# Merge gates of a two-block transformer layer: from direct matmuls to seven block products

## The chip, the cores and the metric

The kernel runs on one core of one Trainium2 chip. The metric is device time of one execution in microseconds (us). The kernel before took 1978.28 us as the median of three runs (1976.41 to 1979.21). Everything is float32.

## The reference, cut to what matters

Two transformer blocks run one after the other over 512 tokens of width 1024. The change lies in the second block, whose attention output `ya` and mLSTM output `ym` are merged by gates:

```python
h = rmsnorm_2(x, norm1_g[l])
proj = h @ w_in[l]            # its last 2048 columns are mg
...
gates = jax.nn.sigmoid(mg + merge_b[l])
u = gates[..., :D_MODEL] * (ya @ w_branch_attn[l]) + gates[..., D_MODEL:] * (ym @ w_branch_mlstm[l])
x = x + u @ w_out[l]
x = x + hier_moe(rmsnorm_2(x, norm2_g[l]), ...)
```

So `mg` is a product of a 512x1024 matrix (the tokens) and a 1024x2048 matrix (weights), and the kernel computes it transposed, as gate columns by tokens.

## The kernel before, in words

Each engine has its own instruction list, written out by hand and kept in order by semaphores. `hT` holds the normed tokens transposed: 8 blocks of 128 model columns by 512 tokens. Weights come in chunks of 2 MB (1024 rows by 512 columns) into a ring of two slots. SP's queue issues these loads in the order in which chunks are used, and each waits until TensorE is done with the chunk that had the slot (`chunk_done`, line 423).

The stage around the change runs in this order on TensorE. The window attention of the second block ends with the matmuls of line 1098. Then comes the mLSTM: `bcast_m`, `qk` and `num` (lines 1043 to 1066), for four heads in two directions, between which VectorE masks (line 2158), weighs (2167) and normalizes and adds (2175 to 2190), and ScalarE takes exponentials. Then `merge_gates(0)` (line 1130) computes the gate columns of output half 0 for both branches: two chunks, in each four groups of 8 matmuls of 128x128 weights by 512 tokens, one group a PSUM bank, which ScalarE reads through a sigmoid into `gates` (line 1580). Within it TensorE turns the two branch outputs (`turn(T_BR)`, line 729 for the transposes), which VectorE copies out (lines 1660 to 1663). Then the branch projections of half 0 (line 1156, two weights of 1 MB in one chunk), with VectorE forming the gated sum `merged` (lines 2224 to 2226). Then `merge_gates(1)` and the branch projections of half 1. The output projection (line 844 in `token_group`) adds to `x`; after it come a norm, the router, and 32 experts whose weights, 6 MB each, are loaded while the expert before is computed.

GpSimd (POOL) has next to nothing to do in this stage: at `hsum_done` 8, the end of the mLSTM, it issues three small DMAs (lines 653 to 655).

The MLP of the first block already uses the scheme that the change brings to the gates. `up_product` (line 860) and `down_product` (line 905) replace the eight products of 2x2 blocks by seven, P1 to P7, of sums of blocks. A product is 8 matmuls of 128x128 by 256. There VectorE forms the sums of weight blocks (for example line 1867, 128x1024 elements) and combines the products from PSUM (for example line 1961), and ScalarE copies P1 out of PSUM (line 1430).

Of the kernel before, what the change touches and what calls it, by code (L numbers as in the profile page):

```python
# [24 lines left out]
ALU = mybir.AluOpType  # L25
# [34 lines left out]
def build(nc, io, out):  # L60
    ctx = ExitStack()
    with ctx:
# [86 lines left out]
        merged = cbuf[:, 0:4096].rearrange("p (c t) -> p c t", c=8)  # L149
        gates = R[:, 0:4096].rearrange("p (b c t) -> p b c t", b=2, c=4)  # L150

# [115 lines left out]
        def kv_view(c):  # L267
# [43 lines left out]
            sem("num_done"), sem("hsum_done"))  # L311
        msq_done, mss_done, mstd_done, mnorm_done = sem("msq_done"), sem("mss_done"), sem("mstd_done"), sem("mnorm_done")
        gate_sig, u_done = sem("gate_sig"), sem("u_done")
        logits_done, r_exp, r_exp_done = sem("logits_done"), sem("r_exp"), sem("r_exp_done")
        h_store = [sem(f"h_store{s}") for s in range(2)]
# [167 lines left out]
        def _(sp):  # L483
# [85 lines left out]
            sp.wait_ge(turn_evac, 40)  # L569
            for j in range(3):  # L570
                sp.dma_start(views[0][j], source[j][0]).then_inc(loads[j][0], 16)

# [31 lines left out]
        def _(pool):  # L604
# [45 lines left out]


            pool.wait_ge(hsum_done, 8)
# [49 lines left out]
        def _(pe):  # L702
# [416 lines left out]
            pe.wait_ge(vext_done, 4)  # L1119
            pe.wait_ge(vone_done, 1)  # L1120
            bcast_m(0)
            qk(0)
            bcast_m(1)
            for r in range(8):
# [4 lines left out]
                num(r)  # L1129
            def merge_gates(half):  # L1130
                for br_ in range(2):
                    c = C_MERGE + 3 * half + br_
                    use_chunk(c)
                    for j in range(4):
                        gs = 8 * half + 4 * br_ + j
                        group(4 + gs % 4, gate_sig, gs + 1)
                        for k in range(KT):
                            ins = pe.matmul(ps[:, 4 + gs % 4, :], ring_view(c, KT, 512)[:, k, j * P:(j + 1) * P],  # L1138
                                            hT[:, k, :], start=(k == 0), stop=(k == KT - 1))
                        ins.then_inc(proj_done, 1)  # L1140
                        if half == 0 and br_ == 1 and j < 2:
                            turn(T_BR, [2 * j, 2 * j + 1])

            bo = 0
            for half in range(2):
                merge_gates(half)
                c = C_MERGE + 3 * half + 2
                pe.wait_ge(turn_evac, 40)
# [165 lines left out]
        def _(act):  # L1314
# [228 lines left out]
            act.wait_ge(acol_ready, 1)  # L1543
            for r in range(8):
                h, dr = r // 2, r % 2
                act.wait_ge(nmd_done, r + 1)
                if r >= 2:
                    act.wait_ge(num_done, r - 1)
                for j in range(NT):
                    a_col = colsb[:, 0, j, 32 * dr + h:32 * dr + h + 1]  # L1550
                    act.activation(E[:, r % 2, j, j * P:(j + 1) * P], nmd[:, r % 2, j, :], ACT.Exp, bias=a_col
                                   ).then_inc(wexp_done, 1)
                    lo, hi = ((j + 1) * P, 512) if dr == 0 else (0, j * P)
                    if lo < hi:
                        act.activation(E[:, r % 2, j, lo:hi], ps[:, 4 + r % 2, lo:hi], ACT.Exp, bias=a_col
                                       ).then_inc(wexp_done, 1)
            act.wait_ge(sig_done, 4)
            act.activation(sigT[:, :, :], sigT[:, :, :], ACT.Sigmoid).then_inc(sig_done, 1)
            act.wait_ge(hsum_done, 8)
            for a in range(NT + 1):  # L1560
                if a < NT:
                    if a >= 2:
                        act.wait_ge(mss_done, a - 1)
                    act.activation(stage[:, a % 2, 0:512], mix[:, a, 512:1024], ACT.Square).then_inc(msq_done, 1)
                if a >= 1:
                    act.wait_ge(mss_done, a)
                    at = 16 + 4 * (a - 1)
                    act.activation(hstd[:, at:at + 4], hss[:, at:at + 4], ACT.Sqrt, bias=epsc[:, 0:1], scale=1.0 / DM
                                   ).then_inc(mstd_done, 1)
            gs = 0  # L1570
            for half in range(2):
                for br_ in range(2):
                    for j in range(4):
                        bank = 4 + gs % 4
                        gs += 1
                        act.wait_ge(proj_done, len(G1) + len(G2) + gs)
                        if half:
                            act.wait_ge(u_done, j + 1)
                        b_ = 8 * br_ + 4 * half + j
                        act.activation(gates[:, br_, j, :], ps[:, bank, :], ACT.Sigmoid, bias=mergeb[:, b_:b_ + 1]  # L1580
                                       ).then_inc(gate_sig, 1)
            for a in range(NT + 1):
# [53 lines left out]
        def _(dve):  # L1636
# [533 lines left out]
            def head_sum(r):  # L2170
# [9 lines left out]
                for b_ in range(2):  # L2180
# [7 lines left out]
                    else:  # L2188
                        then(ins)
                        ins = dve.tensor_tensor(dst, dst, tmp, ALU.add)  # L2190
                        if b_ == 1:
                            ins.then_inc(hsum_done, 1)

            masked_m(0)
            for r in range(8):
# [6 lines left out]
            for a in range(NT + 1):  # L2202
                if a < NT:
                    dve.wait_ge(msq_done, a + 1)
                    at = 16 + 4 * a
                    dve.tensor_reduce(hss[:, at:at + 4], stage[:, a % 2, 0:512].rearrange("p (h e) -> p h e", h=4),
                                      AX.X, ALU.add).then_inc(mss_done, 1)
                if a >= 1:
                    i = a - 1
                    at = 16 + 4 * i  # L2210
                    dve.wait_ge(mstd_done, i + 1)
                    then(dve.reciprocal(hrs[:, at:at + 4], hstd[:, at:at + 4]))
                    mv = mix[:, i, 512:1024].rearrange("p (h e) -> p h e", h=4)
                    dve.tensor_tensor(mv, mv, bc(hrs[:, at:at + 4], DM), ALU.mult).then_inc(mnorm_done, 1)
            dve.wait_ge(sig_done, 5)
            for i in range(NT):
                take_turned(T_BR, i)
            for half in range(2):
                for j in range(4):
# [3 lines left out]
                    a_, b_ = merged[:, bo, :], stage[:, 0, (j % 2) * 512:(j % 2) * 512 + 512]  # L2223
                    dve.tensor_tensor(a_, gates[:, 0, j, :], ps[:, (2 * bo) % 4, :], ALU.mult)
                    then(dve.tensor_tensor(b_, gates[:, 1, j, :], ps[:, (2 * bo + 1) % 4, :], ALU.mult))
                    dve.tensor_tensor(a_, a_, b_, ALU.add).then_inc(u_done, 1)
# [218 lines left out]
```

## Time and profile before

| | us |
|---|---|
| median of 3 runs | 1978.28 |
| time of the profiled execution | 1978.18 |
| span of the profiled execution, first to last instruction | 1976.3 |
| merge gates (both halves) and branch projections, with their turns, 1096.13 to 1265.15 | 169.0 |
| mLSTM ahead of them, about 1037 to 1096 | 59 |

The profile is of one execution. A row that names an engine, a line and tiles gives a busy time. TensorE's rows (PE) come in pairs for float32: a matmul of the code is two records, of which each has its own duration, and they overlap. So the time that a run of matmuls takes is read from the chain of waits, where each piece has its start and its length, and not from the sum of the busy times.

### The profile page before, as it was taken

How to read it: one execution, taken by the hardware profiler on the slowest of the kernel's cores; microseconds unless marked ns; L12 is line 12 of the kernel's file. 1: busy time of each engine (PE TensorE's matmuls, PEld its weight loads, DVE VectorE, ACT ScalarE, POOL GpSimd, SP SyncE). 2: the span in 40 equal slices, each digit the busy share in tenths (PEclk: the TensorE clock that was granted, in tenths of full speed). 3: DMA queues.
4: the chain of work that ended last, by engine and by line, in shares of the span. 5: the costliest groups of instructions: out<-in, count | busy, mean ns of one | idle time of the engine just before them, and what ended most of it. 6: DMA issues, size and time to landing. Idle time of an engine off the chain costs nothing.

```text
span 1976.3 us, 23885 instructions
## 1 busy us (share of the span) xinstructions
PE 1867.3 (94%) x9785; PEld 1062.6 (54%) x9785; DVE 754.6 (38%) x1554; ACT 367.2 (19%) x794; POOL 63.5 (3%) x106
## 2 busy tenths in 40 slices
PE   7999999999999999999998999995999999999994
PEld 3344466568888888654555544454444444444441
DVE  3375666355445343535436220133222222222223
ACT  3332265210000000224434200010111111111110
POOL 0000000000000000100000000000000000000002
PEclk9999968999999999998998899995999999999997
DMA  3532100250222223120111112431999999999994
GB/s 119 119 93 85 69 17 1 85 176 1 85 86 86 90 94 114 55 95 34 43 44 42 57 54 74 191 149 67 355 394 389 387 378 396 398 398 393 392 402 153
DMA packets 83824, 329.17 MB, mean 167 GB/s; under 512 B 7895, under 2 KB 9044, under 8 KB 75564
## 3 DMA queue, kind: packets, MB, share of 16 engines
q1 hardware_dynamic: 71964, 287.45, 38.4%
q0 software_dynamic: 7632, 26.11, 4.9%
q10 hardware_dynamic: 4160, 14.68, 1.9%
q8 instruction: 46, 0.75, 0.2%
q14 instruction: 22, 0.18, 0.0%
HBM read 305.41 MB, written 22.81 MB: 166 GB/s over the span
## 4 chain that ended last, share of the span: by engine, by line
PE 88%; DMA 5%; DVE 3%; ACT 2%; issue 1%; POOL 0%; SPq 0%; POOLq 0%; DVEq 0%; ACTq 0%
PE ps L1212 10%; PE ps L869 10%; PE ps L913 10%; PE ps L761 7%; PE ps L1008 6%; PE ps L844 6%; PE ps L1138 6%; PE ps L1220 5%; PE ps L1240 5%; DMA W<-in_w_expert_up 4%; PE ps L768 3%; PE ps L1156 3%; PE ps L1247 2%; PE ps L797 2%; PE ps L820 1%; PE ps L1019 1%
## 5 line engine op out<-in xcount | busy, mean ns | idle before, releaser
L1212 PE MATMUL ps<-W,yT 128*64 128x512 f32 x1024 | 229.4, 601 | 3.0 <-DMA W<-in_w_expert_up 1.9
L1212 PEld LDWEIGHTS ps<-W,yT 128*64 128x64 f32 x1024 | 72.6, 138 | 144.9 <-issue 143.5
L761 PE MATMUL ps<-hT,W 128*128 128x512 f32 (+1 forms) x336 | 148.4, 600 | 2.2 <-DVE hT L1666 1.3
L1008 PE MATMUL ps<-hT,W 128*128 128x512 f32 x272 | 126.2, 619 | 0.7 <-ACT gb L1467 0.7
L1220 PE MATMUL ps<-W,yT 128*32 128x256 f32 x2048 | 117.1, 380 | 0.0
L1240 PE MATMUL ps<-W,yT 128*64 128x512 f32 x512 | 116.9, 598 | 0.0
L2362 DVE COPY mix<-ps 32x256 f32<-32x256 f32 x128 | 53.9, 421 | 153.7 <-PE ps L1247 152.4
L1138 PE MATMUL ps<-hT,W 128*128 128x512 f32 x256 | 111.2, 595 | 0.0
L761 PEld LDWEIGHTS ps<-hT,W 128*128 128x128 f32 (+1 forms) x336 | 63.0, 190 | 85.2 <-issue 81.9
L1220 PEld LDWEIGHTS ps<-W,yT 128*32 128x32 f32 x2048 | 63.3, 110 | 64.4 <-issue 26.0
L2343 DVE TENSOR_TENSOR yT<-yT,ps 64x512 f32<-64x512 f32 x32 | 22.1, 691 | 193.2 <-ACT yT L1598 193.2
L869 PE MATMUL ps<-yT,cbuf 128*128 128x256 f32 x384 | 85.6, 379 | 2.4 <-issue 2.4
L1008 PEld LDWEIGHTS ps<-hT,W 128*128 128x128 f32 x272 | 53.3, 200 | 63.5 <-issue 62.7
L913 PE MATMUL ps<-cbuf,mix 128*128 128x256 f32 x368 | 81.9, 379 | 0.0
L1138 PEld LDWEIGHTS ps<-hT,W 128*128 128x128 f32 x256 | 48.8, 192 | 60.2 <-issue 60.2
L869 PEld LDWEIGHTS ps<-yT,cbuf 128*128 128x128 f32 x384 | 72.9, 190 | 12.4 <-issue 2.6
L913 PEld LDWEIGHTS ps<-cbuf,mix 128*128 128x128 f32 x368 | 69.9, 190 | 9.5
L1430 ACT ACTIVATE smb<-ps 128x512 f32<-128x512 f32 x10 | 6.0, 595 | 352.6 <-PE ps L913 185.3
L1598 ACT ACTIVATE yT<-ps 64x512 f32<-64x512 f32 x32 | 18.9, 590 | 270.3 <-PE ps L1212 270.3
L1240 PEld LDWEIGHTS ps<-W,yT 128*64 128x64 f32 x512 | 33.9, 136 | 57.0 <-issue 54.8
L1364 ACT ACTIVATE ptb<-ps 32x512 f32<-32x512 f32 x82 | 48.3, 588 | 85.5 <-PE ps L761 84.8
L1247 PE MATMUL ps<-W,yT 128*32 128x256 f32 x1024 | 61.9, 382 | 0.0
(357 smaller groups left out, 2535.3 us busy)
## 6 DMA issues: line engine op xcount, KB each, us to landing
W<-in_w_expert_gate SPq DMA_DIRECT2D x32, 2048.0 KB, 17.8
W<-in_w_expert_up SPq DMA_DIRECT2D x32, 2048.0 KB, 22.3
W<-in_w_expert_down SPq DMA_DIRECT2D x32, 2048.0 KB, 23.4
W<-in_w_in SPq DMA_DIRECT2D x16, 2048.0 KB, 7.7
W<-in_w_up SPq DMA_DIRECT2D x8, 2048.0 KB, 7.5
W<-in_w_down SPq DMA_DIRECT2D x8, 2048.0 KB, 8.0
y_scratch<-mix ACTq DMA_DIRECT2D x32, 384.0 KB, 9.3
W<-in_w_out SPq DMA_DIRECT2D x4, 2048.0 KB, 8.0
```

What stands on the lines that cost most here:

```text
L761: ins = pe.matmul(ps[0:n, bank, :], wv[:, k, j * P:j * P + n], hT[:, k, :], start=(k == 0), stop=(k == KT - 1))
L768: ins = pe.matmul(ps[:, bank, :], hT[:, k, j * P:(j + 1) * P], wv[:, k, :], start=(k == 0), stop=(k == KT - 1))
L844: ins = pe.matmul(ps[:, bank, :], lhs[:, k, i * P:(i + 1) * P], ring_view(c, KT, 512)[:, k, :], start=(k == 0), stop=(k == 7))
L869: ins = pe.matmul(ps[:, bank, 256 * j:256 * j + 256], lhs[:, k, j * P:(j + 1) * P], rhs[:, k, :], start=(j == 0 and k == 0), stop=(j == 1 ...
L913: ins = pe.matmul(ps[:, bank, 256 * t:256 * t + 256], lhs[:, k, t * P:(t + 1) * P], rhs[:, k, :], start=(q == 0 and t == 0 and k == 0), st ...
L1008: ins = pe.matmul(ps[:, bank, :], wv[:, k, j * P:(j + 1) * P], hT[:, k, :], start=(k == 0), stop=(k == KT - 1))
L1138: ins = pe.matmul(ps[:, 4 + gs % 4, :], ring_view(c, KT, 512)[:, k, j * P:(j + 1) * P], hT[:, k, :], start=(k == 0), stop=(k == KT - 1))
L1156: ins = pe.matmul(ps[:, bank, :], ring[c % 2][:, br_ * 2048 + k * 512 + j * P:br_ * 2048 + k * 512 + (j + 1) * P], yT[:, 4 * br_ + k, :], ...
L1212: ins = pe.matmul(ps[64 * part:64 * part + 64, 2, :], xsT[:, x_slot, k, 0:64], wviews[s][part][:, k, :], start=(k == 0), stop=(k == KT - 1))
L1220: ins = pe.matmul(ps[32 * q:32 * q + 32, 3, 0:256], xsT[:, x_slot, k, 64:BLK], wviews[s][q // 2][:, k, 256 * (q % 2):256 * (q % 2) + 256], ...
L1240: ins = pe.matmul(ps[64 * half:64 * half + 64, 4, :], hTa[:, k, :], wviews[s][2][:, k, half * 512:(half + 1) * 512], start=(k == 0), stop= ...
L1247: ins = pe.matmul(ps[32 * q:32 * q + 32, 5, 0:256], hTb[:, k, :], wviews[s][2][:, k, q * 256:(q + 1) * 256], start=(k == 0), stop=(k == 3))
```

## The change: seven products for each chunk of gates, their sums on GpSimd, and all gates first

The gates of a chunk (512 gate columns by 512 tokens, 1024 deep) are computed as seven products of 2x2 blocks, 56 matmuls of 128x128 by 256, where it was 32 of 128x128 by 512. The four sums of weight blocks of each chunk (`gate_w_sums`) and four sums of token blocks, once (`gate_h_sum`), are formed by GpSimd. The token sums may start once the window attention is done; the weight sums of chunk 0 follow them at once. ScalarE copies P1 and P5 from PSUM, VectorE combines the products into the gate's tile (`gate_post`), and ScalarE applies the sigmoid there, in SBUF. The four chunks are now all computed ahead of the branch projections, and the turns of the branch outputs lie behind the third chunk and two products later. On SP's queue the loads of the four gate chunks go before the two of the branch weights, and a wait for `gate_read` 28 stands ahead of the second load of expert weights. The squares of the mLSTM's norm use other halves of `stage` and other semaphores. Some of it, cut:

```diff
+        def gate_view(c):
+            base = cbuf if c < 2 else R
+            return base[:, 2048 * (c % 2):2048 * (c % 2 + 1)].rearrange("p (j t) -> p j t", j=4)
...
-                chunk_done[C_MERGE + 3 * half + br_] = (proj_done, len(G1) + len(G2) + 8 * half + 4 * (br_ + 1))
-            chunk_done[C_MERGE + 3 * half + 2] = (y_done, 8 + 4 * (half + 1))
+                chunk_done[C_MERGE + 2 * half + br_] = (gate_prod, 7 * (2 * half + br_ + 1))
+            chunk_done[C_MERGE + 4 + half] = (y_done, 8 + 4 * (half + 1))
...
+        GATE_READ = dict(P2=1, P6=2, P3=4, P7=5, P4=7)
+        def gate_bank(n):
+            return 4 + n % 4
...
             for half in range(2):
-                c = C_MERGE + 3 * half
-                load(c, cols_of(w2, MG + 512 * half, 512))
-                load(c + 1, cols_of(w2, MG + D + 512 * half, 512))
-                c += 2
+                for br_ in range(2):
+                    load(C_MERGE + 2 * half + br_, cols_of(w2, MG + D * br_ + 512 * half, 512))
+            for half in range(2):
+                c = C_MERGE + 4 + half
                 sp.wait_ge(*chunk_done[c - 2])
+                if half:
+                    sp.wait_ge(y_done, 9)
...
+            def gate_h_sum(n, a, b):
+                pool.tensor_tensor(gate_h[n], a, b, ALU.subtract).then_inc(t_sums, 1)
+                pool.wait_ge(t_sums, 37 + n)
+            def gate_w_sums(c):
+                wv = ring_view(C_MERGE + c, KT, 512)
+                a11, a12, a21, a22 = (wv[:, 4 * k:4 * k + 4, 256 * n:256 * n + 256] for n in range(2) for k in range(2))
+                s1_, s2_, s4_ = gate_w[c // 2]
+                pool.wait_ge(ring_load[(C_MERGE + c) % 2], 16 * ((C_MERGE + c) // 2 + 1))
+                if c % 2:
+                    pool.wait_ge(gate_prod, 7 * c - 1)
+                pool.tensor_tensor(s1_, a21, a22, ALU.add).then_inc(w_sums, 1)
+                pool.wait_ge(w_sums, 64 + 4 * c + 1)
+                pool.tensor_tensor(s2_, s1_, a11, ALU.subtract).then_inc(w_sums, 1)
+                pool.wait_ge(w_sums, 64 + 4 * c + 2)
+                pool.tensor_tensor(s4_, a12, s2_, ALU.subtract).then_inc(w_sums, 1)
+                pool.wait_ge(gate_prod, 7 * c + 3)
+                pool.tensor_tensor(s1_, a11, a21, ALU.subtract).then_inc(w_sums, 1)
+                pool.wait_ge(w_sums, 64 + 4 * c + 4)
...
+            pool.wait_ge(pv_done, len(units))
+            pool.wait_ge(scan_done, 1)
+            gate_h_sum(0, b12, b11)
...
+            for c in range(2):
+                gate_w_sums(c)
+            pool.wait_ge(num_done, 8)
+            pool.wait_ge(wexp_done, 56)
+            gate_w_sums(2)
             pool.wait_ge(hsum_done, 8)
...
+            gate_w_sums(3)
...
+            def gate_product(n):
+                c, name = n // 7, PRODUCTS[n % 7]
+                bank = gate_bank(n)
+                use_chunk(C_MERGE + c)
...
+                if name == "P1":
+                    lhs, rhs = wv[:, 0:4, 0:256], hT[:, 0:4, 0:256]
+                    group(bank, gate_kept, 2 * c + 1)
+                elif name == "P5":
+                    lhs, rhs = w_s[0], h_s[0]
+                    pe.wait_ge(w_sums, 64 + 4 * c + 1)
...
+                for j in range(2):
+                    for k in range(4):
+                        ins = pe.matmul(ps[:, bank, 256 * j:256 * j + 256], lhs[:, k, j * P:(j + 1) * P], rhs[:, k, :],
+                                        start=(j == 0 and k == 0), stop=(j == 1 and k == 3))
+                ins.then_inc(gate_prod, 1)
...
+            for n in range(14):
+                gate_product(n)
+            for n in range(14, 21):
+                gate_product(n)
+            turn(T_BR, [0, 1])
+            for n in (21, 22):
+                gate_product(n)
+            turn(T_BR, [2, 3])
+            for n in range(23, 28):
+                gate_product(n)
...
+            for c in range(4):
+                for n in (7 * c, 7 * c + 2):
+                    gate_keep(n)
+                gate_sigmoids(c, False)
+                gate_sigmoids(c, True)
...
+            for n in range(0, 21):
+                gate_post(n)
             dve.wait_ge(sig_done, 5)
             for i in range(NT):
                 take_turned(T_BR, i)
+            for n in range(21, 28):
+                gate_post(n)
```

`gate_keep` is ScalarE's copy of P1 or P5 (128x512 from PSUM). `gate_sigmoids` are two sigmoids of 128x512 at a time. `gate_post` is one VectorE addition of 128x512 for each of P2, P3 and P4 (a bank of PSUM with a tile of SBUF), and two for P6 and P7, the second of which has both inputs in SBUF. P5 waits for the first weight sum of its chunk, P6 for the second, P3 for the third and P7 for the fourth. The order in a chunk is P1, P2, P5, P6, P3, P7, P4.

## Rows read from the trace of the kernel before

**Rows 1.** The page: busy time by engine, and the chain's shares by engine.
```profile
PE 1867.3 (94%) x9785; PEld 1062.6 (54%) x9785; DVE 754.6 (38%) x1554; ACT 367.2 (19%) x794; POOL 63.5 (3%) x106
...
PE 88%; DMA 5%; DVE 3%; ACT 2%; issue 1%; POOL 0%; SPq 0%; POOLq 0%; DVEq 0%; ACTq 0%
```
**Rows 2.** The chain, gates and branches: start, length, engine, tile, line, records.
```profile
1096.13 35.01 PE ps L1138 x80
...
1139.76 1.75 PE ps L729 x16
...
1155.24 27.47 PE ps L1156 x64
1182.71 54.93 PE ps L1138 x128
```
**Rows 3.** The line of the gates' matmuls.
```profile
L1138 PE MATMUL ps<-hT,W x256: 592/592/1061, 1095.9 to 1237.1; 128*128 128x512 f32 x128
```
**Rows 4.** The chain in the first block's MLP.
```profile
436.99 179.81 PE ps L869 x832
616.80 193.39 PE ps L913 x896
```
**Rows 5.** Stages: window, its length, busy time of each engine, clock, DMA share, GB/s.
```profile
500.00:600.00 100.00, 100.00 (x465) 88.04 (x464) 47.01 (x61) 2.47 (x5) 0.00 (x0) 1.00 0.26 95
...
1037.00:1054.00 17.00, 15.48 (x47) 8.08 (x48) 10.13 (x25) 7.08 (x21) 0.00 (x0) 0.90 0.35 124
...
1110.00:1240.00 130.00, 130.00 (x328) 59.41 (x327) 15.65 (x24) 10.31 (x15) 0.00 (x0) 1.00 0.19 67
```
**Rows 6.** POOL in order of time: start, length, line, operation, tiles.
```profile
0.72 0.20 POOL L613 MEMSET ident<- 128x128 f32 x1 [0.29 <-POOLq L2435]
0.98 0.53 POOL L613 MEMSET cmask<- 128x512 f32 x1
...
4.22 0.29 POOL L625 CAST iot<-mix 128x128 f32<-128x128 int32 x1
...
822.32 3.53 POOL L643 MEMSET yT<- 36x4096 f32 x1
```
**Rows 7.** VectorE and ScalarE in the MLP, grouped by line.
```profile
L1867 DVE TENSOR_TENSOR cbuf<-W 128x1024 f32<-128x1024 f32 x7 | 8.6, 1225 | 14.5 <-PE ps L869 14.5
...
L1961 DVE TENSOR_TENSOR smb<-smb,ps 128x512 f32<-128x512 f32 x8 | 5.5, 688 | 16.3 <-PE ps L869 16.3
...
L1430 ACT ACTIVATE smb<-ps 128x512 f32<-128x512 f32 x10 | 6.0, 595 | 352.6 <-PE ps L913 185.3 <-PE ps L869 147.7 <-DVE smb L1961 19.6
```
**Rows 8.** TensorE in order of time: the window attention's last matmuls.
```profile
1035.95 1.00 PE L1098 MATMUL ps<-W,ptb 128*128 128x64 f32 x8
```
**Rows 9.** VectorE in the mLSTM and at the turns, in order of time.
```profile
1048.96 0.16 DVE L2176 SCALAR_TENSOR_TENSOR mden<-mden 128x4 f32<-128x4 f32 x1
...
1057.39 0.43 DVE L2190 TENSOR_TENSOR mix<-mix,stage 128x256 f32<-128x256 f32 x1
...
1058.18 0.42 DVE L2190 TENSOR_TENSOR mix<-mix,stage 128x256 f32<-128x256 f32 x1
...
1105.32 0.69 DVE L2214 TENSOR_TENSOR mix<-mix,small 128x512 f32<-128x512 f32 x1
...
1141.56 0.69 DVE L1663 TENSOR_TENSOR yT<-yT,W 128x512 f32<-128x512 f32 x1
```
**Rows 10.** SP's queue in order of time: the two first gate chunks.
```profile
989.72 46.80 SPq L492 DMA_DIRECT2D W<-in_w_in  x2
```
**Rows 11.** DMA issues from 980 to 1270: KB each, us to landing.
```profile
W<-in_w_in SPq DMA_DIRECT2D x4, 2048.0 KB, 7.7
...
W<-in_w_branch_mlstm SPq DMA_DIRECT2D x2, 1024.0 KB, 7.4
```
**Rows 12.** ScalarE in order of time: its last norm step, the table load, a sigmoid.
```profile
1104.42 0.30 ACT L1568 ACTIVATE small<-small 128x4 f32<-128x4 f32 x1 [1.11 <-DVE small L2206]
1104.74 1.28 ACT L1580 ACT_TABLE_LOAD   x1
1106.03 0.69 ACT L1580 ACTIVATE W<-ps,mergeb 128x512 f32<-128x512 f32 x1
```

More of the change, by code:

```diff
@@ L570, in _ @@
             for j in range(3):
+                if j == 1:
+                    sp.wait_ge(gate_read, 28)
                 sp.dma_start(views[0][j], source[j][0]).then_inc(loads[j][0], 16)
@@ L1129, in _ @@
                 num(r)
[L1130 to L1142, printed above, removed]
+            for n in range(14):
[8 more added lines that the diff above has]
+                gate_product(n)
             bo = 0
             for half in range(2):
-                merge_gates(half)
-                c = C_MERGE + 3 * half + 2
+                c = C_MERGE + 4 + half
                 pe.wait_ge(turn_evac, 40)
@@ L1543, in _, with weights_out @@
             act.wait_ge(acol_ready, 1)
-            for r in range(8):
+            def weights_out(r):
                 h, dr = r // 2, r % 2
@@ L1556, in _, with gate_keep, gate_sigmoids @@
                                        ).then_inc(wexp_done, 1)
+            def gate_keep(n):
+                c, name = n // 7, PRODUCTS[n % 7]
+                if name not in ("P1", "P5"):
+                    return
+                first = name == "P1"
+                act.wait_ge(gate_prod, n + 1)
+                if c:
+                    act.wait_ge(gate_read, 7 * (c - 1) + (2 if first else 6))
+                act.activation(gate_tmp[c // 2][0 if first else 1], ps[:, gate_bank(n), :], ACT.Copy).then_inc(gate_kept, 1)
+            def gate_sigmoids(c, upper):
+                half, br_ = c // 2, c % 2
+                act.wait_ge(gate_read, 7 * c + (7 if upper else 4))
+                for j in ((2, 3) if upper else (0, 1)):
+                    b_ = 8 * br_ + 4 * half + j
+                    act.activation(gate_view(c)[:, j, :], gate_view(c)[:, j, :], ACT.Sigmoid, bias=mergeb[:, b_:b_ + 1]
+                                   ).then_inc(gate_sig, 1)
+            for r in range(8):
+                weights_out(r)
             act.wait_ge(sig_done, 4)
@@ L1562, in _ @@
                     if a >= 2:
-                        act.wait_ge(mss_done, a - 1)
-                    act.activation(stage[:, a % 2, 0:512], mix[:, a, 512:1024], ACT.Square).then_inc(msq_done, 1)
+                        act.wait_ge(o_ss, NT + a - 1)
+                    act.activation(stage[:, 0, (a % 2) * 512:(a % 2) * 512 + 512], mix[:, a, 512:1024], ACT.Square
+                                   ).then_inc(o_sq, 1)
                 if a >= 1:
-                    act.wait_ge(mss_done, a)
+                    act.wait_ge(o_ss, NT + a)
                     at = 16 + 4 * (a - 1)
                     act.activation(hstd[:, at:at + 4], hss[:, at:at + 4], ACT.Sqrt, bias=epsc[:, 0:1], scale=1.0 / DM
[L1569 to L1581, printed above, removed]
+                                   ).then_inc(o_std, 1)
+            for c in range(4):
[3 more added lines that the diff above has]
+                gate_sigmoids(c, True)
             for a in range(NT + 1):
@@ L2192, in head_sum, with gate_post @@
                             ins.then_inc(hsum_done, 1)
+            def gate_post(n):
+                c, name = n // 7, PRODUCTS[n % 7]
+                first, fifth, acc_, both_ = gate_tmp[c // 2]
+                out_ = gate_view(c)
+                bank = ps[:, gate_bank(n), :]
+                at = 7 * c
+                if name in ("P1", "P5"):
+                    return
+                dve.wait_ge(gate_prod, n + 1)
+                if name == "P2":
+                    dve.wait_ge(gate_kept, 2 * c + 1)
+                    dve.tensor_tensor(out_[:, 0:2, 0:256], wide(first), wide(bank), ALU.add).then_inc(gate_read, 1)
+                elif name == "P6":
+                    dve.wait_ge(gate_kept, 2 * c + 2)
+                    if c:
+                        dve.wait_ge(gate_read, at)
+                    dve.tensor_tensor(acc_, first, bank, ALU.add).then_inc(gate_read, 1)
+                    dve.wait_ge(gate_read, at + 2)
+                    dve.tensor_tensor(both_, acc_, fifth, ALU.add).then_inc(gate_read, 1)
+                elif name == "P3":
+                    dve.wait_ge(gate_read, at + 3)
+                    dve.tensor_tensor(out_[:, 0:2, 256:512], wide(both_), wide(bank), ALU.add).then_inc(gate_read, 1)
+                elif name == "P7":
+                    dve.tensor_tensor(acc_, acc_, bank, ALU.add).then_inc(gate_read, 1)
+                    dve.wait_ge(gate_read, at + 5)
+                    dve.tensor_tensor(out_[:, 2:4, 256:512], wide(acc_), wide(fifth), ALU.add).then_inc(gate_read, 1)
+                else:
+                    dve.tensor_tensor(out_[:, 2:4, 0:256], wide(acc_), wide(bank), ALU.subtract).then_inc(gate_read, 1)
             masked_m(0)
```

51 lines of the change are left out of this document (43 added, 8 removed).

## The prediction, written before the change was run

> **What bounds the kernel now.** I read the page's busy times and its chain by engine first [rows 1]: TensorE is busy 94% of the span and holds 88% of the chain. So a change pays if it takes matmul time away and keeps TensorE fed. The chain in order of time [rows 2] shows the same for this stage: gates, turns and branch projections follow one another as TensorE pieces with no other engine between them, up to the end of the last projection at 1265. Every microsecond less of gate matmuls moves all that comes later, if nothing else becomes late. The part behind it (output projection, router, experts) waits for TensorE's own progress here: SP issues the first expert loads behind `y_done` 16, the end of the branch projections, as before, and all its later times move along with it.
>
> **The matmuls.** Of the gates' matmuls the trace has 256 records [rows 3] for 4 chunks x 4 groups x 8 = 128 calls, so two records are one call. The long piece of the chain, 54.93 us for 128 records or 64 calls [rows 2], gives 0.858 us a call of 512 tokens, and 128 calls take 109.9 us. The new calls are 4 chunks x 7 products x 8 = 224, of 128x128 by 256. The first block's MLP runs this very form: 179.81 us for 832 records (416 calls, 0.4322 us each) and 193.39 us for 896 (448 calls, 0.4317 us) [rows 4]. 224 calls x 0.432 = 96.8 us. The difference is **-13.1 us**. A product is 3.455 us, a chunk 24.2 us. The granted clock is 1.00 in the MLP's stretch and 1.00 in the gates' stretch [rows 5], both the level of 2.4 GHz, so neither term needs a correction. The first call starts behind the mLSTM as before, at 1096.1; the four turns (1.75 us for two [rows 2]) are moved and not changed.
>
> **GpSimd's sums.** There are 4 token sums and 16 weight sums, each with two inputs of 128x1024 in SBUF. The trace of before has no such operation on this engine. From below: a memset costs 0.20 us for 128 columns and 0.53 for 512 [rows 6], so 0.86 ns a column and 0.09 us fixed, which makes 1.0 us for 1024 columns. From above: a cast of 128 columns, one input, takes 0.29 us, 1.56 ns a column after the same fixed part; two inputs at that rate each are 3.3 us, and the longest row of the engine is 3.53 us. I take 2.6 us: the cast is the nearest row, and to its 1.56 ns I add one further stream of the memset's 0.86 ns, (2.42 x 1024) ns + 0.09 us. VectorE needs 1.225 us for the same sum [rows 7]. By the Trainium skill (GPSIMD Engine Reference, Elementwise — side-by-side cycle accounting) an addition of 2048 float32 columns takes 4497 ns on this engine, so an estimate by that page would be 2.25 us, and the sums would end some 2 us sooner.
>
> When must they be there? The window attention ends at 1037.0 [rows 8], and the scan is earlier. Seven sums (four of tokens, three of chunk 0) take 7 x 2.6 = 18.2 us, to about 1055; P5 of chunk 0 starts at 1096.1 + 6.9 = 1103. Chunks 0 and 1 are in the ring by then: their loads went out between 989.7 and 1036.5 [rows 10] and land in 7.7 us [rows 11]. Within a chunk the fourth sum waits for P5 and is due two products later: 6.9 us for one sum. In chunks 1 and 3, which share their buffers with the chunk before, the first waits for P7 of that chunk, and is due behind P4, P1 and P2, 10.4 us later; the second is due at 13.8 us and the third at 17.3 us. Three sums take 7.8 us. So up to 17.3 / 3 = 5.8 us a sum TensorE waits for none of them. Chunk 2 has buffers of its own, and its load is issued when chunk 0 is used up at 1120.3 and landed at 1128. Its sums stand behind chunk 1's fourth (about 1131 + 2.6), and 1134 + 7.8 = 1142 is ahead of 1151. The three small DMAs now stand behind chunk 2's fourth sum, near 1160; what they bring is used beyond 1290. Cost of all this on the path: 0.
>
> **The other queues.** VectorE has 7 operations of 0.69 us in a chunk [rows 7], 4.8 us of 24.2. ScalarE has two copies of 0.6 us [rows 7] and four sigmoids of 0.69 [rows 12], 4.0 us. A bank comes round after four products, so a product's reader has three products, 10.4 us. The first readers are late: ScalarE's norm steps end at 1104.7 and a table load follows [rows 12], VectorE's end at 1106.0 [rows 9]. P1 of chunk 0 (ready 1099.6) is copied by about 1106, and its bank is wanted at 1109.9; P2's at 1113.4. That is the tightest place, and still free. Behind the third chunk, about 1168.7, VectorE turns the tiles: 0.7 + 0.7 + 0.7 us for each of four (the last of them in [rows 9]), in all 7.8 us, while TensorE has two products and then two more before it needs a bank (P2's, four products on) that VectorE holds up. The pair of turns in the middle needs the first pair out of its banks: first pair out by about 1177.5, TensorE there at 1168.7 + 1.75 + 6.9 = 1177.4. I count 0 to 0.5 us. SP: chunk 3 is issued at 1144.5, landed 1152, used 1168.7. The branch weights of half 0 are issued at 1168.7, landed by 1177 (7.4 us [rows 11]), used about 1196.4. Those of half 1 wait for `y_done` 9 at 1203.3, landed about 1211, used at 1223.9. These waits end 13 us or more ahead. The new wait for `gate_read` 28 ahead of the expert loads has ended before `y_done` 16, which stands in front of it. Cost 0.
>
> **The mLSTM, where GpSimd is now busy.** This is the one place where the sums can hurt. From 1037 to 1096 TensorE and VectorE wait for each other in turn, so what delays VectorE is not hidden. The rows at hand show VectorE busy 10.13 of the 17 us from 1037 to 1054 with GpSimd idle [rows 5], and nothing of the two together. Between nothing (the engines don't disturb each other) and all of the sums' 18.2 us (VectorE stands still while GpSimd works) every value is open. I take 0.2 us, on a row: two engines run beside TensorE and ScalarE all through this stage at full durations (the same 0.69 us for 512 columns inside the MLP and at the turns [rows 7, 9]), so a general slow-down isn't a habit of this chip's SBUF. The Trainium skill (SBUF — State Buffer, Who interferes with whom) speaks against a flat zero: VectorE and GpSimd share one read interface, and a VectorE instruction with two SBUF inputs and a GpSimd one that reads SBUF exclude each other for the whole instruction. This is the first rival below. No row of before can agree or disagree.
>
> **Sum.** Own time of the profiled execution 1978.18 (span 1976.3), less 13.1, plus 0.2 for the mLSTM, plus 0.2 for the turns: 1965.5. The median of before is 0.1 us above that execution, so **1965.4**.
>
> **Rivals.**
> *A. Some of VectorE's instructions wait for whole sums.* Those with two SBUF inputs in the window are the small ones near 1049 and the two additions of line 2190 at 1057.4 and 1058.2 [rows 9], the next at 1071. The first have slack: the numerators that need them start 3.5 us later. The additions lie on the chain. They are met if the seven sums run past 1057.4, that is from (1057.4 - 1037.0) / 7 = 2.9 us a sum. At 3.3 us a sum both could wait for one: up to 6.6 us, half of it 3.3. Time 1968.7, at most 1972. For it: 2.9 is within my bounds. Against: my value is below, and only one round of six is met. The same exclusion at line 1663, in the turns, costs up to 1 us through the pair in the middle.
> *B. VectorE stands still for every sum (slower).* If in the mLSTM each sum of GpSimd keeps VectorE out whatever its inputs, the 7 x 2.6 = 18.2 us lie on the chain, less what VectorE idles anyway. In the first 17 us it idles 7 [rows 5], but mostly right before its next instruction is due, so I count the whole: 1978.3 - 13.1 + 18.2 = 1983.4. It is slower than before from a delay of 13.1 us on. For it: the stage is a chain between two engines. Against: memory reads by four engines at once are seen everywhere in the trace at unchanged durations.
> *C. GpSimd sets the pace.* From 5.8 us a sum TensorE waits in chunks 1 and 3, and each further us costs 3 us in each of them; at 7.5 us the gain is gone (2 x (3 x 7.5 - 17.3) = 10.4, about 1.2 for the fourth sums and 2.4 in chunk 2, of 13.1). At 6.5 us: 2 x 2.2 = 4.4, 1969.8. Against it: 3.53 us is the longest row of this engine, for four times the columns [rows 6].
> *D. The products don't run at the MLP's pace,* because the readers come late or the new order collides with a load. Each stall I can place is under 2 us; two of them give 1968.
>
> **Chances.** Forecast 0.72, A 0.12, B 0.05, C 0.03, D 0.08. The forecast's own range is 1963.5 to 1967. Leaving 2 in 10 out, with A and D in it, and 1.5 us of scatter between medians on the low side, the range is 1963.2 to 1970.5. A measurement of this kernel can tell about 0.2%, 4 us, from no change. Faster by more than that: the forecast, A, D and part of C, 0.93. Within: 0.03. Slower: B, 0.04.
>
> **What the changed profile would show.** The products' calls in pieces of 0.432 us each, 24.2 us a chunk, and the last gate piece ending near 1196.5. POOL rows of a sum at 1.0 to 3.3 us, 20 of them. No idle time of TensorE before a product that a POOL row ends. The first product at 1096: a later one means A or B, and VectorE's rows from 1037 to 1060 would show which instruction waited or grew. Wrong would be the prediction if the mLSTM is over 2 us longer, if a sum takes over 5.8 us, or if the part behind 1252 is not the same as that behind 1265 before.

## The result, and the profile after

The changed kernel takes 1963.55 us in the median of 20 runs (1961.31 to 1981.37), the kernel before in as many 1978.07. The ratio is 0.9929, 95% interval 0.991 to 0.9949: faster by 10 to 18 us, where 12.9 were forecast. (A ratio is always to runs of the kernel before taken beside the others.) Three single runs of 2339, 4706 and 4898 us, one each of the twofold and the threefold sums below and of the kernel before, stand in no time or ratio of this text. The profiled execution took 1963.39 us with a span of 1961.6, 14.7 less than the span of before. Runs of one kernel differ by up to 20 us, and most of that goes with the mean granted clock of the run (12 runs of the changed kernel: 1980 and 1982 us at 0.941, 1961 to 1963 at 0.955), which is therefore given where it matters.

The page of the changed kernel, busy times and chain by engine (as [rows 1]):

```profile
PE 1854.4 (95%) x9977; PEld 1098.7 (56%) x9977; DVE 779.6 (40%) x1582; ACT 371.2 (19%) x802; POOL 111.0 (6%) x126
...
PE 92%; DVE 3%; ACT 2%; issue 1%; DMA 1%; POOL 0%; POOLq 0%; DVEq 0%; ACTq 0%
```

TensorE is busy 13 us less in a span that is 15 us shorter, so its share has risen. GpSimd has 48 us more work and no share of the chain. The chain through gates, turns and branch projections (start, length, engine, tile, line, records), to set beside [rows 2]:

```profile
1096.81 73.22 PE ps L1212 x336
1170.03 1.75 PE ps L786 x16
1171.78 6.91 PE ps L1212 x32
1178.69 1.75 PE ps L786 x16
1180.43 17.27 PE ps L1212 x80
1197.70 54.95 PE ps L1247 x128
1252.65 0.02 issue
1252.67 0.69 DVE cbuf L2363
```

No piece of another engine stands between the products: 448 records in 97.40 us, with 73.22 / 168 = 0.436 us a call in the piece that begins at the lower clock and 17.27 / 40 = 0.432 in the last. The branch projections are one piece of 54.95 us, two of 27.47 and 27.48 before. From the first gate matmul to the end of the last projection it is 1252.67 - 1096.81 = 155.86 us, where it was 1265.15 - 1096.13 = 169.02.

GpSimd in order of time (start, length, line; 20 sums, of which the first and the last of the mLSTM and some of the products stand here):

```profile
1037.74 2.35 POOL L677 TENSOR_TENSOR W<-hT 128x1024 f32<-128x1024 f32 x1 [208.32 <-PE ps L1155]
...
1052.33 2.36 POOL L691 TENSOR_TENSOR yT<-W,smb 128x1024 f32<-128x1024 f32 x1
1107.95 2.34 POOL L693 TENSOR_TENSOR smb<-W 128x1024 f32<-128x1024 f32 x1 [53.27 <-PE ps L1212]
1118.40 2.35 POOL L687 TENSOR_TENSOR smb<-W 128x1024 f32<-128x1024 f32 x1 [8.11 <-PE ps L1212]
1120.84 2.69 POOL L689 TENSOR_TENSOR smb<-smb,W 128x1024 f32<-128x1024 f32 x1
```

A sum is 2.35 us and the next starts 2.43 us after it. The seven early ones end at 1054.7. Later it is GpSimd that waits for TensorE, 53 and 8 us in these rows. VectorE, however, has rows that are not as they were (1118.99 and 1171.99; each of these forms takes 0.69 us elsewhere in the same stage):

```profile
1118.27 0.69 DVE L2323 TENSOR_TENSOR yT<-yT,ps 128x512 f32<-128x512 f32 x1 [2.76 <-PE ps L1212]
1118.99 2.32 DVE L2325 TENSOR_TENSOR cbuf<-yT 128x512 f32<-128x512 f32 x1
...
1171.27 0.68 DVE L1768 TENSOR_TENSOR yT<-ps,gcol 128x512 f32<-128x512 f32 x1
1171.99 2.84 DVE L1769 TENSOR_TENSOR yT<-yT,W 128x512 f32<-128x512 f32 x1
```

Both have two inputs in SBUF and began while a sum of GpSimd ran (the second at 1171.99, beside a sum from 1171.93 to 1174.28). The first ended at 1121.31, 0.56 us after that sum's end at 1120.75, and the sum behind it took 2.69 us instead of 2.35. The neighbours that read PSUM and one tile of SBUF kept 0.68 and 0.69 us. Two more rows of this form were longer, 1.20 and 2.29 us (1136.26 and 1167.34). All of it was hidden: no piece of the chain above grew by it.

Where the time went, from the starts of TensorE's pieces in the profiles (us):

| | mLSTM to first gate matmul | gates and branches, with the pause behind them | to the first expert | experts and end | span |
|---|---|---|---|---|---|
| before | 59.03 | 171.30 | 104.73 | 604.35 | 1976.3 |
| changed | 59.01 | 158.14 | 105.38 | 601.48 | 1961.6 |
| order alone | 59.04 | 171.29 | 104.56 | 600.86 | 1973.0 |
| changed, a second profile | 59.01 | 158.14 | 105.39 | 601.91 | 1966.3 |

Ahead of the mLSTM the changed kernel is 0.7 us later, in code that is the same.

### The profile page after: what moved, and what is told of

The parts are those of the page before. It is cut to its first block, busy times and chain, and to the rows that moved or that the text cites. A ratio compares the mean times of both kernels' runs of the same rounds, so it can differ in the third digit from the quotient of the medians.

```text
span 1961.6 us, 24364 instructions
## 1 busy us (share of the span) xinstructions
PE 1854.4 (95%) x9977; PEld 1098.7 (56%) x9977; DVE 779.6 (40%) x1582; ACT 371.2 (19%) x802; POOL 111.0 (6%) x126
## 4 chain that ended last, share of the span: by engine, by line
PE 92%; DVE 3%; ACT 2%; issue 1%; DMA 1%; POOL 0%; POOLq 0%; DVEq 0%; ACTq 0%
PE ps L1303 12%; PE ps L926 10%; PE ps L970 10%; PE ps L818 7%; PE ps L1065 6%; PE ps L1311 6%; PE ps L1331 6%; PE ps L901 6%; PE ps L1212 5%; PE ps L1338 3%; PE ps L825 3%; PE ps L1247 3%; PE ps L854 2%; PE ps L877 1%; PE ps L1076 1%; PE ps L1293 1%
## 5 line engine op out<-in xcount | busy, mean ns | idle before, releaser
L1065 PE MATMUL ps<-hT,W 128*128 128x512 f32 x272 | 126.4, 620 | 0.7 <-ACT gb L1558 0.7
L1065 PEld LDWEIGHTS ps<-hT,W 128*128 128x128 f32 x272 | 53.3, 200 | 63.6 <-issue 62.8
L901 PE MATMUL ps<-W,cbuf 128*128 128x512 f32 x128 | 57.1, 607 | 2.1 <-DVE cbuf L2365 2.1
L970 PE MATMUL ps<-W 128*128 128x256 f32 x256 | 56.6, 379 | 0.0
```

Source lines behind the costliest of these rows:

```text
L901: ins = pe.matmul(ps[:, bank, :], lhs[:, k, i * P:(i + 1) * P], ring_view(c, KT, 512)[:, k, :], start=(k == 0), stop=(k == 7))
L970: ins = pe.matmul(ps[:, bank, 256 * t:256 * t + 256], lhs[:, k, t * P:(t + 1) * P], rhs[:, k, :], start=(q == 0 and t == 0 and k == 0), st ...
L1065: ins = pe.matmul(ps[:, bank, :], wv[:, k, j * P:(j + 1) * P], hT[:, k, :], start=(k == 0), stop=(k == KT - 1))
```

## The experiments

**The changed kernel again.** No edit.

> The changed kernel, unaltered. Matmul count theory: gates, turns and branch projections take 155.9 us where the kernel before takes 169.0, so 13.1 us less. The profile of the changed kernel had a span shorter by 14.7 us, of which 2.65 us lay in the experts, where this change touches nothing. If those are scatter, the experts here differ from run to run by 1 to 3 us and the median gain stays between 12.5 and 15.5 us. Rival: the shorter gate stage leads the expert loads into a better rhythm, and the experts are again 2 to 3 us shorter than in the kernel before.

Measured: median 1963.52 us (12 runs) against 1977.55, 14.0 less and inside the expected 12.5 to 15.5; ratio 0.9941 (0.9914 to 0.9968). The stage is 158.14 us to the hundredth. The experts took 601.91 us; with the order-alone kernel's 600.86, which leaves the change's products out, the 604.35 of before is the odd one. Its expert phase has waits for a load that the changed one doesn't have, of 1.9 us in three places, near its end. So the 2.65 us are scatter and no gain. In all sessions ten runs of the kernel before and nine of the changed one had a recorded mean clock of 0.955; their medians are 1975.34 and 1962.22, 13.1 us apart.

**The order alone.**

```diff
-            for n in range(14):
-                gate_product(n)
...
+            for gs in range(12):
+                gate_group(gs)          # 8 matmuls of 128x128 by 512, as before
+            turn(T_BR, [0, 1])
+            gate_group(12)
+            turn(T_BR, [2, 3])
+            for gs in (13, 14, 15):
+                gate_group(gs)
```

> One part of the change alone: all four gate chunks ahead of the branch projections, with the new order of loads and turns, but as direct matmuls of 512 tokens (16 groups of 8), the sigmoid from PSUM, and no sums. Matmul count theory: 128 calls x 0.858 us as before, so the stage from the first gate matmul to the last branch projection takes 169.0 us, and the time is that of the kernel before within 1 us. Rival: the order brings part of the gain (fewer changes of chunk, loads that come earlier): 2 us or more less than before.

Measured: 1978.45 us (12 runs), ratio 1.0007 (0.9978 to 1.0036); stage 171.29 us against 171.30. The order is worth nothing that could be seen, and the 13.2 us belong to the products.

**GpSimd longer in the mLSTM.**

```diff
+                again(2, gate_h[n], a, b, ALU.subtract)    # the sum once more, ahead of the one that counts
                 pool.tensor_tensor(gate_h[n], a, b, ALU.subtract).then_inc(t_sums, 1)
```

> Each of the four token sums on GpSimd is formed twice, so 11 sums of 2.43 us run from 1037.7 to about 1064.4 instead of 7 to 1054.7. They now meet the second head sum at 1056.8 to 1059.3, which is on the chain and has four VectorE instructions with two SBUF inputs, and the start of the third. If such an instruction waits for the end of the running sum (0 to 2.4 us each), the first gate product starts 4 to 8 us later, at 1101 to 1105, and the time is 1968 to 1972; instructions with one SBUF input keep their durations. If the engines don't exclude each other, the first product stays at 1096.8 and the time at 1963.5. If VectorE stands still for every sum, those with one SBUF input grow as well and the delay is 9 us or more.

Measured: mLSTM to first product 65.35 us, 6.3 more and inside the expected 4 to 8. The time was not: a median of 1974.37 us (10 runs, ratio 0.9989, 0.996 to 1.0018) where 1968 to 1972 were expected. Three runs at a clock of 0.954 or 0.955 took 1966.7 to 1967.3, 5 us above the changed kernel's 1962.22; four at 0.941 or 0.942 took 1980.7 to 1985.8. Why more of its runs had the lower clock is open; the profile too came to the mLSTM 7.4 us late, with a lower clock in the first block's attention (0.78 for 0.84 from 200 to 360), so the span says little. A head sum is VectorE's normalizing and adding for one head in one direction. VectorE in order of time in that kernel, its second head sum, and the sums of GpSimd beside it:

```profile
1064.45 0.16 DVE L2296 SCALAR_TENSOR_TENSOR mden<-mden 128x4 f32<-128x4 f32 x1
1064.64 2.33 DVE L2297 TENSOR_TENSOR mden<-mden,gb 128x4 f32<-128x4 f32 x1
1067.01 0.18 DVE L2298 RECIPROCAL mden<-mden 128x4 f32<-128x4 f32 x1
1067.23 0.42 DVE L2303 TENSOR_TENSOR stage<-ps,mden 128x256 f32<-128x256 f32 x1
1067.68 1.97 DVE L2310 TENSOR_TENSOR mix<-mix,stage 128x256 f32<-128x256 f32 x1
1069.58 0.41 DVE L2303 TENSOR_TENSOR stage<-ps,mden 128x256 f32<-128x256 f32 x1
1070.02 2.11 DVE L2310 TENSOR_TENSOR mix<-mix,stage 128x256 f32<-128x256 f32 x1
```

```profile
1064.62 2.34 POOL L698 TENSOR_TENSOR smb<-W 128x1024 f32<-128x1024 f32 x1
1067.04 2.34 POOL L701 TENSOR_TENSOR smb<-smb,W 128x1024 f32<-128x1024 f32 x1
1069.45 2.40 POOL L704 TENSOR_TENSOR yT<-W,smb 128x1024 f32<-128x1024 f32 x1
```

An operation over four columns (`mden` with `gb`) takes 2.33 us where it took 0.17: its two inputs lie in SBUF and a sum started at 1064.62, 0.02 us before it. The two of 256 columns take 1.97 and 2.11 instead of 0.43. Together that is 5.4 us, on the chain. What reads PSUM with one SBUF tile kept 0.42. This is rival A's mechanism, and it is not rival B.

The rest of the 6.3 us is TensorE's clock, in both directions. Pieces of its chain behind that head sum, and the last numerators:

```profile
1072.28 4.64 PE ps L1134 x20
1076.92 2.00 PE ps L1117 x2
1078.92 4.98 PE ps L1123 x8
...
1108.06 2.47 PE ps L1134 x20
```

In the changed kernel the same four pieces took 3.62, 1.51, 3.63 and 4.64 us. After the head sum TensorE ran at half the clock (0.50 from 1070 to 1080), and the delay grew from 5.4 to 8.5 us by the last numerators; those then found the full clock and gave 2.2 us back. So the exclusion itself costs 5.4 us here, the clock behind it 3.1, and the 2.2 that came back were in no expectation.

By the Trainium skill (SBUF — State Buffer, Who interferes with whom) a VectorE instruction with two SBUF inputs contends with a GpSimd instruction that reads SBUF, while one with at most one SBUF input, outside the modes that use two ports, does not; these rows agree.

**GpSimd longer during the products.** `again(2, ...)` and `again(3, ...)` ahead of each of the four weight sums of chunks 1 to 3.

> Each weight sum of chunks 1 to 3 is formed twice, 4.86 us. Four in a queue are 19.4 us for the 20.7 us until P7 is due, so TensorE waits nowhere: gate stage 156 to 157.5 us, time 1963.5 within 2 us. Ahead of the limit of 5.2 us a sum there is only 1.3 us left in a chunk; VectorE's additions with two SBUF inputs, which hold a sum up by 0.3 us each, should not use it up. If the cost of a longer sum grows evenly instead of from a limit on, this kernel pays about a third of what the threefold one pays.

> Each weight sum of chunks 1 to 3 is formed three times on GpSimd, so one takes 7.3 us. The four sums of a chunk stand in a queue, 29.2 us for a round of products of 24.2 us. Counted from the end of P7 of the chunk before: third sum ready at 21.9 us for a P3 that is due at 17.3, fourth at 29.2 for a P7 that is due at 20.7, so TensorE stands 8.5 us in each of chunks 1 and 3; in chunk 2, whose sums follow at once, 1.2 + 3.8 = 5.0 us. Gate stage 22 us longer (about 180 us), time about 1985 (1980 to 1990). By the rule of the prediction, which counted three sums and left the fourth out of the queue, it would be about 13 us. If sums of GpSimd can't hold TensorE up, 1963.

Measured, twice: stage 158.10 us for 158.14, and no wait of TensorE for GpSimd, as expected. The time is weak evidence: the median of five runs is 1965.64 us (ratio 0.9963, 0.9917 to 1.0009), two at a clock of 0.955 took 1960.51 and 1962.16, and two at 0.941 took 1980 and 1982, where the kernel before takes 1993 to 1995. Thrice: 1987.39 us (10 runs), ratio 1.0034 (1.0004 to 1.0063), inside the expected 1980 to 1990; stage 183.18 us, 25.0 more. TensorE's waits in the whole stage (who waited for whom: total, times, longest):

```profile
PE ps L1226 <- POOL W L707: 4.8, 2, 3.9
PE ps L1226 <- POOL W L704: 4.2, 2, 2.9
PE ps L1226 <- POOL yT L704: 3.9, 1, 3.9
...
PE ps L1226 <- POOL smb L701: 1.2, 1, 1.2
PE ps L1226 <- POOL smb L707: 1.0, 1, 1.0
```

These are 15.1 us and not 22. Most of the rest is the clock: waits of 3.9, 3.9 and 2.9 us are each followed by a product at half of it (the granted clock is 0.50 from 1160 to 1163), so three of the products take 6.15, 6.44 and 6.73 us for 3.62, 8.5 us more in all. That doesn't mean that such a wait is paid one and a half times. In chunks 1 and 3 the slow product is P3, and GpSimd was still at the fourth sum, so P7 only waited less behind it (0.99 and 0.87 us). The chain holds one of the three, P7 of chunk 2, between two sums of GpSimd:

```profile
1193.89 2.35 POOL W L707
1196.29 6.45 PE ps L1226 x16
...
1202.88 2.36 POOL W L682
```

Its 2.8 us lengthened the stage. Counted at the start of P7, with that of the changed kernel beside it, the chunks added 9.2, 5.7 and 10.1 us, where 8.5, 5.0 and 8.5 were expected. Chunk 3 holds those 2.8 us; the expectation had also left out the two pairs of turns in it (3.5 us that TensorE does while GpSimd works), and sums of 2.7 us instead of 2.35, beside VectorE's additions, took part of that back. So the cost begins at a limit and is zero before it, as expected; the limit lies between 4.9 and 7.3 us a sum.

**All sums on VectorE, in gaps.**

```diff
                 weigh(r)
+                if 1 <= r < 7:
+                    next(sums)          # one dve.tensor_tensor of 128x1024
                 if r >= 1:
                     head_sum(r - 1)
+            next(sums)
             head_sum(7)
```

> The seven products with every sum on VectorE, none on GpSimd: the seven sums that are due first stand one each in the gaps of the mLSTM in which VectorE waits for the numerators (1.6 to 4.8 us before each of its seven later head sums, for a sum of 1.22 us), the others between its readings of the products. If GpSimd is only one of several places that are hidden, the first product starts at 1096.8 as in the changed kernel and the time is the same within 1 us (1963.5). Rival: VectorE is needed at once in those gaps, each sum delays the chain by part of its 1.2 us, and the kernel is 2 to 8 us slower than the changed one.

> The kernel with every sum on VectorE once more, against a fresh set of runs. It was 4 us below the changed kernel in the median, although its matmuls and waits are the same: its profile had the last numerators of the mLSTM at the full granted clock (2.47 us against 4.64 us) and no half clock after the pause ahead of the output projection. If the clock is granted to it more often (mean clock 0.957 in 6 of 11 runs, against 1 of 32 of the changed kernel), the median is again 1958 to 1961 and most runs show 0.957. If that was luck of one session, the median is that of the changed kernel, 1963 +- 1.

Measured: 1959.29 us (11 runs), ratio 0.9923 (0.9895 to 0.9952), then 1959.19 (6 runs), ratio 0.989 (0.9852 to 0.9928). Neither 1963.5 nor slower: 4 us faster than the changed kernel (1963.52 in the same session), and with the kernel of the next experiment the best of all versions run. The gaps hide the sums, but the price isn't quite zero: TensorE's waits for VectorE grow from 1.61 to 1.68 us. What it gains is in the last numerators (TensorE in order of time, first this kernel, then the changed one):

```profile
1092.97 2.47 PE L1088 MATMUL ps<-W 128*128 128x129 f32 x20 [1.74 <-DVE mix L2257]
```

```profile
1092.17 4.64 PE L1120 MATMUL ps<-W 128*128 128x129 f32 x20 [1.75 <-DVE mix L2289]
```

The same 20 records take half the time. The granted clock is 1.00 from 1092 on here, and 0.50 from 1090 to 1095 in the changed kernel, as in the kernel before. The mLSTM is 57.29 us instead of 59.01, the stage behind it 157.40 instead of 158.14, since its first product starts at full clock too. In this profile the output projection also keeps 1.00 behind the pause ahead of it, where the two main kernels fall to half for some 3 us. The first piece of that projection is 1.70 us shorter by it (the changed kernel, then this one):

```profile
1254.74 50.03 PE ps L901 x112
```

```profile
1252.67 48.33 PE ps L869 x112
```

The mean clock is 0.957 in 6 of 11 and 3 of 6 runs, against 1 of 32 of the changed kernel. It is no mark of this placing alone, though: 6 of 34 runs of the kernel before had 0.957 in the same session.

**Only the first seven on VectorE.** As above for the four token sums and the first three of chunk 0; the other thirteen stay with GpSimd.

> A cross of the two: the seven sums that are due first stand on VectorE in the gaps of the mLSTM, the other thirteen stay on GpSimd during the gate products. If the clock depends on what the mLSTM's stretch looks like (a few tenths of a us more between TensorE's bursts), this behaves as the kernel with all sums on VectorE: mean clock 0.957 in most runs, median 1958 to 1961. If it depends on GpSimd being at rest during the products, it behaves as the changed kernel: 0.952 to 0.955, median near 1963. The gate stage itself takes 155.9 to 157.4 us in either case.

Measured: 1959.52 us (6 runs), ratio 0.9887 (0.9849 to 0.9925); mLSTM 57.28 us, last numerators 2.47 us, stage 157.40. So it is the mLSTM's stretch and not GpSimd's rest during the products. The mean clock was 0.958 in two of the six runs and 0.953 or 0.955 in four, so the expected "most runs" was missed while the median was met.

**The same sums as idle work in the kernel before.**

```diff
+            def idle_sum():
+                then(dve.tensor_tensor(unused, g12, g11, ALU.subtract))
```

> The kernel before, with seven sums of 128x1024 on VectorE in the gaps of the mLSTM whose results nobody reads. They do no useful work. If the 4 us by which the kernels with the first sums on VectorE are below the changed kernel come from the clock (the sums shift TensorE's bursts in the mLSTM by some 0.3 us in all, and the last numerators then find the full clock, 2.47 us instead of 4.64 us), this kernel gets them too: last numerators at 2.5 us, the first gate matmul 1.7 us nearer to the mLSTM's start (57.3 instead of 59.0 us), and a median 2 to 4.5 us below the kernel before. If they come from GpSimd's rest (no exclusion on the shared reads), nothing is gained here, since GpSimd rests in the kernel before too: 1977.5 or up to 2 us more.

Measured: mLSTM 57.25 us for 59.03, last numerators 2.47 for 4.64, stage 170.57 for 171.30. So 2.5 us of the profile are bought by work whose result nobody reads, which shows that this part comes from the clock and not from GpSimd's rest. The output projection fell to half the clock as in the kernel before (49.98 us for its first piece). The time shows no gain: 1976.58 us against 1976.48, ratio 1.0004 (0.9983 to 1.0026). Three of its 12 runs and one of 18 of the kernel beside it had a clock of 0.942 to 0.944, with which both take over 1991. Here the expectation failed: 2 us or more were not to be seen in the median, and whether all runs have the 2.5 us of the profile is not known.

**The first seven on VectorE, in one block.** The seven sums stand ahead of `masked_m(0)`.

> All sums on VectorE, the seven that are due first in one block ahead of the mLSTM's first masking, not in its gaps. Seven sums of 1.225 us are 8.6 us, less the 0.5 us by which they overlap with the first matmuls: the mLSTM is about 8 us longer (65 to 67.5 us from its first matmul to the first product), and the time 8 us above the kernel with the sums in the gaps, near 1967. That would be the price of the place, with the same work. If TensorE's own work in the first heads covers a part, 3 to 6 us.

Measured: 1966.54 us (4 runs), ratio 0.9946 (0.9932 to 0.996); from the mLSTM's first matmul to the first product 64.87 us, 7.6 above the kernel with the gaps. TensorE stands 7.37 us at once, behind the second pair of broadcasts. That is the price of the place. Here, too, the last numerators took 2.47 us and the projection's first piece 48.33.

## Why the prediction was right

The time, 1963.55, lies within the range of 1963.2 to 1970.5, near its lower end; 1965.4 was forecast. (The last step of that sum has the wrong sign: 1965.5 for the execution and 0.1 more for the median give 1965.6. It changes nothing.)

*The matmuls.* -13.1 us predicted from the MLP's pace, 169.02 - 155.86 = 13.16 measured, with the order shown to be worth nothing. This term is the whole gain of the stage.

*GpSimd's sums.* 2.6 us taken between 1.0 and 3.3, 2.35 measured, 2.43 from start to start. The cast's 1.56 ns a column with one further stream was 0.25 us too much. The end of the seven was predicted for 1055 and came at 1054.7, in a profile that reached the mLSTM 0.7 us later. The estimate of 2.25 us, half of the 4497 ns that the Trainium skill gives for 2048 columns (GPSIMD Engine Reference, Elementwise — side-by-side cycle accounting), was nearer, 0.10 us too low.

*The other queues.* All waits that were to be hidden are hidden. The pair of turns in the middle was counted with up to 0.5 us and cost nothing, although VectorE's first pair was held up by 2.1 us (the row at 1171.99): it was out at 1176.7, TensorE came at 1178.7. The 0.2 us were too much: the time of 1177.5 for the first pair fits only if it is charged with the 7.8 us of all four tiles, where two unhindered ones take 3.9 (1179.16 to 1183.10). The exclusion at this place, named under rival A, was right in kind.

*The mLSTM.* 0.2 us taken, 0.0 measured (59.01 for 59.03). It was not for lack of a mechanism. The seven sums ended 2.1 us before the head sum they would have met; that is luck of place, as the doubled token sums show. The first head sum, which they did meet, got off as well: its four-column operation started at 1049.86, 0.02 us ahead of a sum, and kept its 0.17 us.

*Rival A* had the right mechanism, and its price was right by accident: up to 6.6 us were expected of the two additions, and in the kernel with doubled token sums they paid 3.2 us, the four-column operation 2.2, the lower clock 3.1, and 2.2 came back, which makes 6.3. The prediction had called the small ones slack. In these rows a held instruction of four columns pays as much as one of 256; what counts is that it has two SBUF inputs and when in the running sum it starts.

*Rival B* is refuted by every row with one SBUF input, and by the mLSTM's 59.01 us for 59.03 with seven sums in it.

*Rival C* was mis-sized. Three sums within 17.3 us gave a limit of 5.8 us; the fourth sum stands in the same queue, is due at 20.7 us, and makes it 20.7 / 4 = 5.2 us. The threefold sums cost 25.0 us where the prediction's rule gives about 13. That the queue counts is shown by P7's waits for the fourth sum, 0.99, 3.88 and 0.87 us, each behind a P3 that had waited for the third; the clock adds 2.8 us. That the limit is 5.2 in chunk 1 is worked out, and only its bounds of 4.9 and 7.3 were run.

*The sum.* 1.5 us more than the 13.16 are gone from the profile's span: -2.65 in the experts, +0.65 between the stage and the first expert, +0.7 ahead of the mLSTM, -0.2 at the end. For the experts two more profiles show scatter, and so they do for the start of the mLSTM (1037.25 and 1041.85). The +0.65 is not scatter by these profiles: it came again to 0.01 us in the changed kernel (105.39) and is absent with the order alone (104.56). 0.42 of it are the router's first 32 records, 6.66 us for 6.25, in a stretch that falls to the half clock; the rest is a wait for a DMA, 5.99 us for 5.76, which lies between 5.59 and 6.09 in all profiles. What moved the clock there is open.

The 4 us that the gap version gains have their places in the profiles: 1.7 us in the mLSTM, 0.7 in the first product, 1.7 in the output projection. Idle sums in the kernel before show that the first two follow from the sums' place in the mLSTM. Open is what decides the clock behind the pause ahead of the output projection. It fell to half there (50.03 or 49.98 us) in both main kernels, with the order alone, with the twofold sums and with the idle ones; it kept 1.00 (48.33 us) in the three kernels with the first sums on VectorE, with the doubled token sums and with the threefold weight sums. In the idle-sum kernel the last numerators had the full clock and this piece had not, with the threefold sums it was the other way round, so the one doesn't bring the other.

## What to carry to other kernels

When a chain is one engine's matmuls, read their pace from the same form elsewhere in the trace and count calls; that sum was right to 0.1 us. Moving elementwise work to GpSimd was free here only while no VectorE instruction with two SBUF inputs, however small, stood on the chain beside it; list those by their place in time, and add up GpSimd's whole queue against the last sum that is due. And look for gaps of the faster engine first: here they held the sums at half their duration.

## What the runs showed of the hardware that was not expected

- A VectorE operation of four columns with two SBUF inputs took 2.33 us instead of 0.17 beside a GpSimd sum, and the sum that starts while a held instruction still runs is itself 0.3 us longer (2.69 for 2.35).
- A shift of TensorE's bursts by 0.07 us each, seven sums in gaps, moved the last numerators from half to full clock (2.47 us) in all four profiles with that placing; the six in which the mLSTM's chain was as before all had 4.64 us. The two in which TensorE stood for 7 us at once in the mLSTM (7.01 with the doubled token sums, 7.37 with one block) had 2.47 as well, so the gaps are one way to it among several.
- Waits of 3.9 and 2.9 us amid products were followed by a product at half clock (6.15 and 6.73 us for 3.62); waits of 1.2 us were not (3.72).
